# First stage of a two-block transformer kernel: value products of one row block ahead of the query and key projection

## The reference, cut to what matters

```
a_qk, a_v, a_o, a_g, b_q, b_k, b_v = split(x @ w_in, [1024, 512, 512, 16, 512, 512, 512])
a_qk = silu(conv5(a_qk))            # depthwise over tokens; gives a_q and a_k
gates = a_g + gate_b                # input and forget gates of the mLSTM
h = mlstm(a_q, a_k, a_v, gates)     # 4 heads, 2 chunks of 128 tokens, both directions
```

## Time and profile before

| | us |
|---|---|
| median of 3 runs | 2232.96 (2231.99 to 2238.97) |
| the profiled execution's own time | 2237.7 |
| its span | 2235.9 |
| PE busy | 2208.5 |
| DVE busy | 1440.7 |
| ACT busy | 1073.7 |
| POOL busy | 104.9 |

### The profile page before, as it was taken

The page is one execution under the profiler, slowest core; times in us unless marked ns, Lnnn a source line. Parts: engine busy times, 40 slices in busy tenths (PEclk is TensorE's granted clock), DMA queues, the critical chain, the costliest instruction groups (busy, mean ns, idle before and its releaser), DMA issues.

```text
span 2235.9 us, 38334 instructions
## 1 busy us (share of the span) xinstructions
PE 2208.5 (99%) x16065; PEld 2050.7 (92%) x16065; DVE 1440.7 (64%) x1691; ACT 1073.7 (48%) x1314; POOL 104.9 (5%) x174
## 2 busy tenths in 40 slices
PE   9999999999999999999999999999999999999998
PEld 9989899888999989998999998998998999998997
DVE  6885655577755565556875676566556776677555
ACT  4554444357354443443656454443443565455442
POOL 2310000000000000000011000000000012000000
PEclk9999999999999999999999999999999999999999
DMA  7656556663555565665553655665565553565553
GB/s 248 209 183 208 169 177 192 198 177 131 196 166 174 189 223 174 196 223 182 177 158 99 219 206 179 198 213 183 189 198 194 180 169 116 189 228 168 189 180 122
DMA packets 348523, 411.90 MB, mean 184 GB/s; under 512 B 11452, under 2 KB 280952, under 8 KB 348224
## 3 DMA queue, kind: packets, MB, share of 16 engines
q1 hardware_dynamic: 339184, 377.19, 52.5%
q0 software_dynamic: 9168, 32.26, 4.5%
HBM read 406.51 MB, written 5.00 MB: 184 GB/s over the span
## 4 chain that ended last, share of the span: by engine, by line
PE 93%; DVE 4%; ACT 2%; issue 1%; DMA 1%; DVEq 0%; ACTq 0%; SPq 0%
PE bank L364 92%; ACT wh L1259 1%; DMA raw<-in_w_mix_in 1%; DVE x L1924 0%; DVE z L1919 0%; DVE stat L1885 0%; DVE front_l L1810 0%; DVE wl L1810 0%; DVE z L1883 0%; PE bank L1225 0%; DVE em_l L1810 0%; ACT em_h L1259 0%; DVE xl L1844 0%; DVE nmax L2274 0%; PE bank L1229 0%
## 5 line engine op out<-in xcount | busy, mean ns | idle before, releaser
L1810 DVE TENSOR_TENSOR wl<-raw,wh 128x2048 fp32r<-128x2048 f32 (+1 forms) x352 | 762.3, 2171 | 512.5 <-ACT wh L1259 441.4
L364 PE MATMUL bank<-xl,wh 128*128 128x256 f32 x3144 | 879.3, 280 | 5.0 <-issue 3.4
L364 PE MATMUL bank<-xh,wl 128*128 128x256 f32 x3144 | 870.9, 277 | 0.0
L364 PE MATMUL bank<-xh,wh 128*128 128x256 f32 x3144 | 870.9, 277 | 0.0
L1259 ACT ACTIVATE wh<-raw 128x2048 fp32r<-128x2048 f32 (+1 forms) x352 | 637.6, 1817 | 322.3 <-PE bank L364 293.8
L364 PEld LDWEIGHTS bank<-xl,wh 128*128 128x128 f32 x3144 | 591.0, 188 | 12.1 <-issue 7.0
L364 PEld LDWEIGHTS bank<-xh,wl 128*128 128x128 f32 x3144 | 590.0, 188 | 2.0 <-issue 1.4
L364 PEld LDWEIGHTS bank<-xh,wh 128*128 128x128 f32 x3144 | 590.1, 188 | 0.2
L364 PE MATMUL bank<-wl,hh 128*128 128x512 f32 x528 | 205.9, 390 | 0.0
L364 PE MATMUL bank<-wh,hh 128*128 128x512 f32 x528 | 205.5, 389 | 0.0
L364 PE MATMUL bank<-wh,hl 128*128 128x512 f32 x528 | 205.4, 389 | 0.0
(11 more groups left out here) (395 smaller groups left out, 3148.4 us busy)
## 6 DMA issues: line engine op xcount, KB each, us to landing
raw<-in_ffn_w_in SPq DMA_DIRECT2D x80, 1024.0 KB, 5.2
raw<-in_w_mix_in SPq DMA_DIRECT2D x56, 1024.0 KB, 5.3
raw<-in_ffn_w_gu SPq DMA_DIRECT2D x40, 1024.0 KB, 5.3
raw<-in_ffn_w_out SPq DMA_DIRECT2D x40, 1024.0 KB, 5.0
raw<-in_ffn_w_down SPq DMA_DIRECT2D x20, 1024.0 KB, 5.1
raw<-in_mem_wkv SPq DMA_DIRECT2D x16, 1024.0 KB, 5.5
raw<-in_even_w_in SPq DMA_DIRECT2D x13, 1024.0 KB, 6.5
raw<-in_w_branch SPq DMA_DIRECT2D x24, 512.0 KB, 3.4
```

The costliest lines, as they stand in the source:

```text
L364: ins = pe.transpose(o, a, b) if transpose else pe.matmul(o, a, b, start=start, stop=stop)
L1810: dve.tensor_tensor(part_of(t, 1), raw_tile(t), part_of(t, 0).bitcast(F32), ALU.subtract)\
```

## The change

The first half of the value projection's weights becomes the first weight tile of the program. PE multiplies it with row block 0 while row block 1 is not transposed yet, then transposes block 1, waits for its parts, and multiplies it with block 1. The query/key tiles and the gates follow. The second half of the value products comes behind `aqk` 3, and `cum` behind that. SP issues the rows of block 0, the first weight tile, and then the rows of block 1. ACT and DVE convert block 0, tile 0, block 1 in that order. The warming matmuls change from 24 and 14 to 11 and 22. The number of products and their operands are the same.

```diff
-WARM = 24
-WARM_X = 14
+WARM = 11
+WARM_X = 22
...
-            await_parts()
+            for t in range(TB):
+                take(("av", t), "acc")
+            h, l = weights([W[0:512, 1024:1536]], 4)
+            for t in range(TB):
+                if t:
+                    x_to_T(0, [t])
+                await_parts()
+                tok = slice(t * P, t * P + P)
+                for k in range(4):
+                    three(ps[where[("av", t)][0]][:, :], xh[:, k, tok], xl[:, k, tok], h[:, k, :], l[:, k, :], k == 0, False)
+            owed[0] += 1
             o = take(("aqk", 0))
...
             aqk_tile(3)
 
-            def av_step(k0):
-                proj_N([("av", t) for t in range(TB)], W, 1024, 512, KC, xh, xl, [k0], "acc")
-
-            av_step(0)
+            h, l = weights([W[512:1024, 1024:1536]], 4)
+            for t in range(TB):
+                tok = slice(t * P, t * P + P)
+                for k in range(4, KC):
+                    three(ps[where[("av", t)][0]][:, :], xh[:, k, tok], xl[:, k, tok], h[:, k - 4, :], l[:, k - 4, :],
+                          False, k == KC - 1, ("av", t) if k == KC - 1 else None)
+            owed[0] += 1
...
-            av_step(4)
...
 (PE, behind the first warming matmuls)
-        x_to_T(0)
+        x_to_T(0, [0])
...
 (ACT and DVE alike)
-        x_to_T(0)
+        x_to_T(0, [0])
+        split_to(0)
+        x_to_T(0, [1])
...
 (SP)
-        for t in range(TB):
+        def rows_in(t):
             sp.dma_start(x[:, t, :], A["x"][0, t * P:t * P + P, :]).then_inc(sig(f"x_loaded{t}"), 16)
+
+        rows_in(0)
         for t, (pieces, nk, w, _, _) in enumerate(weight_tiles):
...
+            if t == 0:
+                rows_in(1)
```

## The result

| | kernel before | changed kernel |
|---|---|---|
| median of the runs | 2235.34 us (2231.99 to 2238.97, 7 runs) | 2242.87 us (2241.05 to 2245.47, 7 runs) |
| profiled execution (span) | 2237.7 (2235.9) | 2241.86 (2240.1) |

What follows compares the result with a forecast made beforehand. PE was taken as the bound, busy 2208.5 of 2235.9 us. Start and block 1 +1.3, stall at `decay_cols` +2.7, POOL +0.1 sum to +4.1: 2237.1 us on the median of 2232.96, range 2232 to 2242.

Steps and rivals of the forecast that it cites:

- The start: PE's first product at 12.7 instead of 14.12, a head start of 1.45 us, between 0.2 and 2.1.
- the eight transposes put off the rise of the clock: Warm-up: transposes may not count as TensorE activity; a rise 2 us later would cost about 0.3.
- Block 1 in the middle: Between block 0's and block 1's products PE transposes and waits for parts: 2.77 us; less the head start, +1.3.
- The reordered stage: First stage: 24 products moved to the front make every query/key tile end 5.60 + 1.3 = 6.9 us later.
- The chain of DVE: DVE's convolutions: their end moves by 6.9 - 0.5 = 6.4, so `decay_cols` comes at 62.6 instead of 56.20.
- the wait of 0.52: DVE's wait before 33.67: goes, because the tile behind has been asked for by then; taken as -0.5.
- a rival at 0.10: Second value half's weight tile lands late, 13.2 us after issue; 1.4 in DVE's chain, 0.8 by a mask: +6.2, 2239.2.
- The masks: POOL's masks against DVE's convolutions: three losses again (0.55, 0.8, 0.8), difference +0.1, bounds -1.6 and +0.8.
- The stall: PE reaches `decay_cols` at 60.0 and stands 2.7 us; `C` starts at 62.7 instead of 58.73, +4.0.
- Behind the first stage: After `qk_ready`, DVE is 4.2 behind PE's 4.0; the rest of the span shifts as a whole.
- The clock: Rival: a PE gap (first product, block 1, `decay_cols`) drops the clock, 2.6 us each; one gives +6.7; chance 0.13.
- That whatever lets PE start sooner is gained: Whole kernel: PE busy 2208.5 of 2235.9 us, so first-stage delays reach the end nearly one for one and earlier starts are gained.

Runs made afterwards that it cites:

- Experiment 10: Changed kernel with POOL's loads brel0, boneh and rv put off until the eighth weight tile is converted: 2239.17 us, ratio 1.0007 to the kernel before.
- Experiment 7: Changed kernel without POOL's four mask additions, the stores kept: 2240.88 us, ratio 1.0016 to the kernel before.
- experiment 12: Changed kernel run and profiled once more, unedited: 2243.38 us, ratio 1.0028 to the kernel before.
- experiment 1: Kernel before with only the warming numbers changed, 11 and 22 instead of 24 and 14: 2236.26 us, ratio 0.9999.
- experiment 8: Kernel before with warming numbers 11 and 22 and POOL's constant loads released by the first converted weight tile: 2238.06 us, ratio 1.0006.
- experiment 9: Kernel before with warming numbers 11 and 22 and POOL's loads brel, boneh and rv put off until the seventh weight tile is converted: 2235.69 us, ratio 0.9992.
- experiment 3: Changed kernel with block 1 transposed behind the second warming group, ahead of block 0's products: 2241.23 us, ratio 1.0024 to the kernel before.
- experiment 11: Changed kernel with block 1 transposed early, `ao` 1 ahead of `C`, `tab` between `ao` 0 and `ao` 1, three POOL loads put off: 2235.28 us, ratio 0.9994.
- experiment 5: Changed kernel with the `tab` matmul behind `ao` 0 instead of directly behind `cum`: 2245.19 us, ratio 1.0034 to the kernel before.
- experiment 2: Changed kernel with the old warming numbers 24 and 14, so the new order alone: 2246.58 us, ratio 1.0053 to the kernel before.
- experiment 6: Changed kernel with all POOL's constant loads released by the first converted weight tile: 2245.27 us, ratio 1.0033 to the kernel before.
- experiment 4: Changed kernel with `ao` 1 ahead of the wait for `decay_cols`, DVE's look-ahead there cut by one tile: 2240.28 us, ratio 1.0023.

## Why the prediction was right, and where it was not

**The start** (forecast 12.7): 12.54. The first tile landed at 1.65 + 6.5 = 8.1 against a forecast of 8.2. `WARM_X` ended at 11.15 instead of 12.0, with no effect, since the tile was the later of the two. The prediction feared that the eight transposes put off the rise of the clock; this trace can't tell, since the 22 passes of `WARM` took 4.13 us instead of the 4.7 of the lower level, so the rise came before the transposes.

**Block 1 in the middle** (2.77): 15.37 to 18.14 is 2.77.

**The reordered stage** (+6.9 for what hangs on PE): the copy of `aqk` 1 +6.96, `cum` +6.99.

**The chain of DVE** (+6.4, `decay_cols` at 62.6): this is the step with a term that was mis-sized. I took the wait of 0.52 before the seventh tile as gone, "because the tile behind has been asked for by then". It became 1.30, because being asked for isn't being there: the tile took 13.1 us in company. +0.8 in place of -0.5 is 1.3 us, and `cc_` came at 63.76, +7.7. I had this as a rival at 0.10, with the very duration of the earlier trace rows; the rows spoke for it, and it should have had the larger part. The rival's own sum (+6.2) had also a fourth mask in the chain, and that did not come; that it is so near the 6.3 of the runs is luck in this part. Experiment 10 isolates the tile: 1.23 us at DVE's conversion.

**The masks** (three losses again, about 2.1 us, difference +0.1): three, 2.1. Experiment 7 confirms both cause and size.

**The stall** (forecast: PE at 60.0, `C` at 62.7, +4.0): `C` at 63.99, +5.26, the surplus from the late tile. Where the clock didn't fall in `ao` 0 (experiment 12) PE reached the wait at 63.85 - 3.69 = 60.16, as forecast.

**Behind the first stage** ("the rest of the span shifts as a whole"): in this profile not quite. Of +5.56 at 170 us, 1.4 is missing at the end, in stretches that vary by more than this between executions. So the profiled +4.2 that meets the forecast of +4.1 is two errors that cancel: +1.3 from the tile, which recurs, and -1.4 of chance further on. The first stage is the better measure. Its landmark is 5.56 and 6.64 later in the two profiles of the changed kernel, and by the runs the loss is 6.3 (4.2 to 8.3): the first stage accounts for it, and the forecast was some 1.5 to 2.5 too low there.

**The clock.** The rival put the fall in one of the three waits, at 2.6 us, decisive from one on. It did happen, once in the first stage in each of the two profiles: in one within `ao` 0, where the wait for `decay_cols` hid it, in the other ahead of `C`, where it cost 1.45 us (5.29 instead of 3.84) on top of the wait. The per-run record agrees: the mean granted clock is 0.9978 in the 6 runs of experiment 12 and 0.9984 in the 27 of the kernel before beside them, a difference worth about 1.3 us by my estimate (0.0006 of 2240), a rough one, as each run's clock is recorded to 0.001. Further on, 10 of the 14 profiles show a short fall or two, at places that vary (such as 275, 1375 and 2055 us), of about 1.6 us each. Three of them are of the old order (experiments 1, 8 and 9), and the two of the changed kernel itself show none there, so these falls aren't shown to be part of the loss. How often they come in an execution that isn't profiled stays open.

**That whatever lets PE start sooner is gained** was the sentence that misled most. The page's 99% holds for the whole; in the first stage PE is the bound only by small margins against DVE and the weight transfers. PE ran 1.5 us earlier in experiment 1 and nothing came of it, and 3.1 us earlier in experiment 3 and 0.5 came of it. With the waits of DVE mended, the changed order gives 0.9994 and the old order with the same warming numbers 0.9992. Neither can be told from the kernel before, nor from the other; both can be told from the changed kernel. At the landmark the old order is 1.66 us ahead of the kernel before (experiment 9) and the changed one 0.83 (experiment 11), so no gain from the order shows. What gain there may be comes from the warming numbers and the loads.

## What to carry to other kernels

Before moving a block of work to the front, list what the second engine's chain receives from the blocks behind it: its end moves by the whole length of the block, and only its margin at the consumer is free. For a prefetch, ask at what time it *lands* and in what company it is issued; "it was issued early enough" costs a microsecond when a row of the same trace shows 13 us for such a transfer. An earlier start is worth something only if the next wait down the line gets earlier with it, so undo or mend that wait in the same experiment.

## What the runs showed of the hardware that I had not expected

- A wait of PE can cost more than itself. Waits of 3.69, 3.74 and 4.05 us ahead of `C` (experiments 12, 5 and 3) were followed by 32 passes in 5.29, 6.08 and 6.28 us, those of 0.30, 1.52 and 2.10 us by the usual 3.84. The wait of 4.05 cost 6.5 in all. How long a wait must be isn't shown: in the three runs with the short waits the clock had just fallen and come back within `ao` 0, and a wait of 2.13 us in experiment 8, behind the gates' products of 16 columns, was followed by a fall that cost 1.7.
- The clock can also fall while PE is busy. Where the small matmuls of `cum` (4 and 8 columns) and of `tab` (32 rows) stand together, 2.3 us of them, the clock fell 0.1 to 1.0 us behind them in 5 of 8 profiles (the changed kernel and experiments 2, 6, 7 and 10; not 3, 4 and 12); in the 6 where about 5.6 us of other products lie between the two, it never fell there. The changed kernel shows it in one execution and not in the other, so it isn't the order of the instructions alone; what else decides was not settled.
- An early load can do harm as well as a late one. POOL's loads, put early, made another tile late (experiment 8) or brought all the masks into the chain (6); with three of them (`brel`, `boneh` and `rv`) put late, no tile was late for DVE (9, 10). In the old order their place was worth 4.0 us at `cc_` (57.41 against 53.44).
